# Moving the scaling and storing of the first row half one period earlier, and the pooled sums of a unit ahead of the gating of the one before

## The reference

```python
for g, w in enumerate(POOL_SIZES):            # 2, 4, 8, 16; 128 channels each
    upper = c[:, 1:]                          # c: running sum of the mixer's input
    lower = jnp.pad(c, ((0, 0), (w - 1, 0), (0, 0)))[:, :S]
    outs.append((upper - lower) / cnt - xg[:, :, g])
y = jnp.einsum('bsgd,gde->bsge', pooled, w_pool).reshape(B, S, C_WIDTH) * scale
...
x = x + jnp.einsum('bse,ed->bsd', mix, w_out[l])
return _rmsnorm(x, final_g)                   # needs the squares of a whole row
```

## Time and profile before

| what | value |
|---|---|
| median of 3 runs | 1189.27 us (1188.85 to 1189.97) |
| the profiled execution, its own time | 1189.71 us |
| its span in the trace | 1187.9 us |
| PE busy | 1169.2 us, 98% of the span |
| DVE busy | 872.3 us, 73% |
| ACT busy | 491.5 us, 41% |
| DMA | 354.98 MB, 299 GB/s in the mean |
| mean granted clock of PE | 0.996 of full speed |

### The profile page before, as it was taken

The page is one execution under the profiler, slowest core; times in us unless marked ns, Lnnn a source line. Parts: engine busy times, 40 slices in busy tenths (PEclk is TensorE's granted clock), DMA queues, the critical chain, the costliest instruction groups (busy, mean ns, idle before and its releaser), DMA issues.

```text
span 1187.9 us, 15646 instructions
## 1 busy us (share of the span) xinstructions
PE 1169.2 (98%) x5862; PEld 954.5 (80%) x5862; DVE 872.3 (73%) x1150; ACT 491.5 (41%) x863; POOL 37.5 (3%) x76
## 2 busy tenths in 40 slices
PE   9999999999999999999999999999999999999995
PEld 8878878888888888888888877778878888888884
DVE  5799939677777767888776797988777445586674
ACT  6375564524534333447333362423333432223235
POOL 0012100000000000000000000000000000000000
PEclk9999999999999999999999999999999999999998
DMA  9999999687864476996567686799997648896878
GB/s 349 418 375 415 394 416 346 203 308 286 320 226 160 163 268 243 347 341 202 190 231 261 206 336 232 255 323 363 420 412 302 248 175 342 321 413 226 310 280 326
DMA packets 103435, 354.98 MB, mean 299 GB/s; under 512 B 10656, under 2 KB 17856, under 8 KB 92224
## 3 DMA queue, kind: packets, MB, share of 16 engines
q1 hardware_dynamic: 98432, 336.15, 76.7%
q0 software_dynamic: 4928, 17.83, 3.7%
HBM read 282.37 MB, written 71.57 MB: 298 GB/s over the span
## 4 chain that ended last, share of the span: by engine, by line
PE 81%; DVE 9%; DMA 7%; issue 1%; SPq 1%; ACT 1%; POOL 0%; DVEq 0%; ACTq 0%
PE n_bank L1911 25%; PE n_bank L1912 25%; PE n_bank L1913 25%; DMA x_parts<-s_ring 3%; PE e_bank L2062 2%; DVE w_lo L1344 2%; PE t_bank L2090 2%; PE t_bank L2073 2%; DMA xc<-x_t_dram 2%; DVE w_b L1469 1%; DMA s_ring<-m_parts 1%; DMA s_ring<-x_parts 1%; DVE s_ring L1353 1%; DMA xa<-x_t_dram 1%; DVE va L1526 0%
## 5 line engine op out<-in xcount | busy, mean ns | idle before, releaser
L1006 ACT ACTIVATE w_hi<-w_b 128x1024 fp32r<-128x1024 f32 (+1 forms) x200 | 197.8, 1033 | 421.1 <-PE n_bank L1913 365.3
L1911 PE MATMUL n_bank<-s_ring,w_hi 128*128 128x512 f32 x896 | 357.5, 399 | 1.3 <-DMA s_ring<-x_parts 1.3
L1913 PE MATMUL n_bank<-s_ring,w_lo 128*128 128x512 f32 x896 | 349.0, 390 | 0.0
L1912 PE MATMUL n_bank<-s_ring,w_hi 128*128 128x512 f32 x896 | 349.0, 389 | 0.0
L1344 DVE TENSOR_TENSOR w_lo<-w_b,w_hi 128x1024 fp32r<-128x1024 f32 (+1 forms) x200 | 231.9, 1198 | 102.9 <-ACT w_hi L1006 102.7
L1911 PE MATMUL n_bank<-w_hi,s_ring 128*128 128x512 f32 x672 | 262.1, 390 | 2.0 <-DMA s_ring<-m_parts 0.9
L1913 PE MATMUL n_bank<-w_hi,s_ring 128*128 128x512 f32 x672 | 261.5, 389 | 0.0
L1912 PE MATMUL n_bank<-w_lo,s_ring 128*128 128x512 f32 x672 | 261.5, 389 | 0.0
L1911 PEld LDWEIGHTS n_bank<-s_ring,w_hi 128*128 128x128 f32 x896 | 168.2, 188 | 41.7 <-issue 2.5
L1913 PEld LDWEIGHTS n_bank<-s_ring,w_lo 128*128 128x128 f32 x896 | 168.2, 188 | 35.7
L1912 PEld LDWEIGHTS n_bank<-s_ring,w_hi 128*128 128x128 f32 x896 | 168.3, 188 | 35.3 <-issue 2.2
(11 more groups left out here) (210 smaller groups left out, 945.3 us busy)
## 6 DMA issues: line engine op xcount, KB each, us to landing
s_ring<-x_parts SPq DMA_DIRECT2D x224, 512.0 KB, 6.0
w_b<-w_b_dram SPq DMA_DIRECT2D x76, 1024.0 KB, 10.6
s_ring<-m_parts SPq DMA_DIRECT2D x96, 512.0 KB, 6.1
x_parts<-s_ring POOLq DMA_DIRECT2D x32, 512.0 KB, 11.4
x_parts<-s_ring SPq DMA_DIRECT2D x24, 512.0 KB, 14.5
m_parts<-stage SPq DMA_DIRECT2D x20, 512.0 KB, 8.6
rows<-x_dram SPq DMA_DIRECT2D x8, 1024.0 KB, 11.3
residual<-x_dram SPq DMA_DIRECT2D x6, 1024.0 KB, 9.5
```

The lines of the kernel that those rows point to most:

```text
L1006: sc.activation(w_hi[:, J % 2, part], w_source(J)[:, part], ACT.Copy).then_inc(hi_done, 1)
L1911: pe.matmul(psum_out, stat[0], mov[0], start=first, stop=False)
L1912: pe.matmul(psum_out, stat[0], mov[1], start=False, stop=False)
L1913: return pe.matmul(psum_out, stat[1], mov[0], start=False, stop=last)
```

## The change

`finish_first` moves on ACT from the end of step 96 to step 95, right behind `split_hi(96)`, and on DVE from the end of step 96 to step 95, right behind `split_lo(96)` and ahead of the weight sum and the adds. On SP the four stores of the first half move from the end of step 96's turn to the end of step 95's, which has `load_s(97)` before it and step 96's residual load behind it. In pooling, `pool_half(u + 1)` is called ahead of `pool_gate(u)`, and its wait for PE's reading of `aux` stands just ahead of the write of `aux`, no longer ahead of the window sums.

```diff
@@ SP
-                if n == CHUNKS - 2:
+                if n == CHUNKS - 3:
 
                     for c, y, done, count in ((0, y11[PAIR_O], y_scaled, 4), (1, y12[PAIR_O], y_scaled, 8),
                                               (2, y11[PAIR_O + 1], y_normed, 4), (3, y12[PAIR_O + 1], y_normed, 8)):
@@ ACT
                 elif J + 1 < TOTAL and J not in SUM_S3:
                     split_hi(J + 1)
+                if J == step(PAIR_U, 11):
+                    finish_first()
...
-                if J == step(PAIR_O + 1, 12):
-                    finish_first()
@@ DVE, pool_half
-                if u >= 1:
-                    ve.wait_ge(pool_ready, u)
                 window = POOLS[j]
                 src = pool_x
                 for m in range(j + 1):
...
                     src = dst
+                if u >= 1:
+                    ve.wait_ge(pool_ready, u)
                 last = ve.scalar_tensor_tensor(out=aux[:], in0=src[:, HIST:HIST + HS], scalar=1.0 / window,
@@ DVE, the loop
                 if STEPS <= J + 1 < TOTAL:
                     split_lo(J + 1)
+                if J == step(PAIR_U, 11):
+                    finish_first()
...
                 u = J - POOL_AT
+                if 0 <= u + 1 < 8:
+                    pool_half(u + 1)
                 if 0 <= u < 8:
                     pool_gate(u)
-                if 0 <= u + 1 < 8:
-                    pool_half(u + 1)
...
-                if J == step(PAIR_O + 1, 12):
-                    finish_first()
```

## The result

The changed kernel takes 1196.65 us (median of 4 runs, 1196.44 to 1197.86); the kernel before, run beside it, 1189.11 us. The ratio is 1.0069, with a 95% interval of 1.0056 to 1.0082: slower, by 7.5 us between the medians. The forecast was 1196.0 us, 6.7 us more. The profiled execution has a span of 1194.9 us where 1194.6 was worked out.

What follows compares the result with a forecast made beforehand. PE is busy 98%, but the end is a store backlog. Residual landing 1173.7 + 7.5 + 0.9 + 11.1 + 1.4 = 1194.6 span, +6.7 us, so 1189.27 + 6.7 = 1196.0 us; range 1189.0 to 1198.5.

Steps and rivals of the forecast that it cites:

- The order in SP's queue, and the landing: SP's last residual load waits behind four stores, 4.19 MB or 11.1 us, so its landing moves from 1162.6 to 1173.7.
- From the residual to the end: After the last residual lands: 7.5 us chain, 0.9 to busy DMA, 11.1 of stores, 1.4 to the end; landing + 20.9.
- The term of 7.5 us: DVE and ACT, sixth residual add to the second half's first store: adds, squares, root and scaling, as before, 7.5 us.
- DVE's part and PE's stall: Moved block takes 4.0 us on DVE in step 95; PE stalls 0.1 and 1.9 us, covered by the late residual.
- the fourth rival: Tail: stall's clock or slower root eats the 6 us cover, or stores run at 0.35; 1199 to 1201 us; chance 0.04.
- Pooling: DVE's order of pooled tile and gate gains 0, within 0.1 us either way; PE's wait stays 1.0 us.
- the load passes the stores: Rival at the last residual load: it lands before 1167.0, stores follow without a hole; 1186.9 us at best; chance 0.08.
- it shares the engines with them: Rival: the residual load passes the stores in part, landing 1166 to 1170; 1188.3 to 1192.3 us; chance 0.12.
- The third: Rival: residual near 1164, only PE's stall matters, 3.5 us plus some 2 us of clock; 1189 to 1191 us; chance 0.04.
- the two ceilings: For the four stores' rate: 435 GB/s for the fabric, about 358 for a core's memory; the forecast took 0.376 MB a us.

Runs made afterwards that it cites:

- the run with the residual first: Changed kernel with the four first-half stores put back behind the last residual load, scaling staying in step 95; 1188.69 us, ratio 0.9998.
- the run with the order alone: Kernel before, with only SP's four stores put ahead of the last residual load in step 96's turn, scaling and pooling untouched; 1201.91 us, ratio 1.0107.
- the run on POOL's queue: Changed kernel with the last residual load issued by POOL on its own queue, with its own semaphore; 1190.75 us, ratio 1.0015.
- the cut version: Kernel before, with root and ACT's scaling moved to step 95, DVE's scaling left in step 96, residual load first; 1186.94 us, ratio 0.9984.

## Why the prediction was right

**The order in SP's queue, and the landing.** 1173.7 was forecast, 1173.6 measured. The mechanism is shown from both sides: restoring the order alone gives the time back, making the order alone costs 12.9 us (with SP's wait for the scaling in it), and the same load in another queue is early. The size hit partly by luck, because errors cancel. The execution reached step 95 0.9 us earlier, so that the landing, counted from there, came 0.8 us later than forecast. The slots' loads of step 97, which SP had issued ahead of the stores, ran at only 0.274 and 0.244 MB a us from 1154 to 1158, against 0.379 and 0.344 in the kernel before; the last of them landed at 1159.9, when by the earlier start it should have been 1159.0. Behind them the stores ran at 0.409, where I took 0.376. Against the slower start stands the faster rest. That SP would be held in issuing was not in the forecast; as the load queued behind the stores anyway, it is not seen to have cost anything.

**From the residual to the end.** 20.9 us forecast, 21.3 measured. The term of 7.5 us from the add to the first store came out at 7.5 (1173.58 to 1181.10), and so did 0.9 to a busy DMA; the bytes took 11.2 for 11.1 (1182.0 to 1193.2), and the rest is in the last one, 1.7 us (1193.2 to 1194.9) for 1.4. Counted from the start of step 95 the end came 1.2 us later than forecast, 0.8 of it in the landing and 0.4 in this term; the execution's earlier start hides 0.9, which leaves the span 0.3 us above the forecast. The median is 0.65 us above it, less than the four runs lie apart (1.4 us).

**DVE's part and PE's stall.** The block took 3.9 us (1145.34 to 1149.25) for 4.0: ACT did load its table before it was needed, at 1144, and its scales ended 1.75 us before its next split, where 1.7 was worked out. PE waited 0.17 and 1.60 us where 0.1 and 1.9 were worked out. The granted clock stayed at 1.00 through the wait, so the clock's share of the fourth rival was nothing. The wait was covered by the late residual, as said; once the residual was early it was the next thing to set the end, seen in the run with the residual first. There I had priced the gain of the earlier stores without setting the chain from PE's last bank against it, and so missed by 1 us.

**Pooling.** Forecast at 0 with 0.1 us either way for the instructions; measured 0.2 us more on PE, and PE's wait of step 60, forecast to stay at 1.0 us, became 1.27. Its mechanism stands: PE needs both, and the later one decides.

**The rivals.** That the load passes the stores is ruled out by the run with the order alone; that it shares the engines with them is how it goes between two queues, but not within one. Its price (L near 1166 to 1170, 1188.3 to 1192.3 us) is what the run on POOL's queue gave, 1190.75. The third needed a residual that is not late; the run with the residual first has that and the same stall of PE, and it took 1188.7 us, since the stall was 1.8 us and not 3.5 and cost no clock. The fourth is out as well: the last bank's add came only at 1183.8, behind the residual's chain, with the cover not used up, and the stores ran at 0.41; what was slow, for 0.9 us in all, were the slots' loads.

For the order in one queue say more than the prediction took from them. By the two landings alone the loads could also have shared the engines, which were full then. But the weight load between them landed at 892.1 (880.23 + 11.9), 2.4 us behind the store and 2.5 us ahead of the load of u: one after the other.

## What to carry to other kernels

Before a store is moved ahead, look at what is queued behind it on the same issuer: a load that the critical path still needs then waits for all its bytes, here 4.2 MB and 11 us, and, if the store itself must wait for its data, for that too. The wait shows in the trace of a far-off engine. Put the load first, or give it a queue of its own, and only then look for the gain. And take an early finish apart: the part on an idle engine (ACT's scales) could move for nothing, while the part on DVE pushed the weights of the next step by 3.9 us (their split starts 16.9 us behind ACT's split of step 95, before 13.0).

## What the runs showed of the hardware that I had not expected

Stores of the same shape ran at two rates. Where they followed loads without a pause, they went at 0.40 to 0.41 MB a us: 409 GB/s in the changed kernel from 1160 to 1166, 408 in the cut version at 1170 to 1172, with a DMA share of 1.05. Where they started on idle engines they went at 0.36 to 0.39: 376 GB/s in the changed kernel after 1182, and all through the backlog of the kernel before (384 at 1176 to 1178). The faster rate is above the lower of the two ceilings from which the prediction made its estimates; the measured rate decides. No run here tells the cause of the two rates.

Loads slowed down when stores stood behind them in the same queue. From 1154 to 1158 the changed kernel moves at 274 and 244 GB/s. These are still the slots' loads of step 97: they land by 1159.9 and the first store only at 1162.5, 2.6 us before the second. So of the 10 us by which the stores are issued earlier, only 5 are left at the first landing (1167.5 in the kernel before). Over the same windows these loads ran at 379 and 344 GB/s in the kernel before and at 326 and 381 with the residual first, where no store is issued by then; with the residual on its own queue, where the stores stand behind them again, at 266 and 227. Why is not shown.

SP takes longer over an issue when much is under way: the two stores from 1154.19 took it 5.2 us and the residual load 2.5, where the residual load took 0.4 us in the kernel before. No semaphore accounts for it, since the tiles of these stores were scaled by 1149.3 and the fifth residual add was done by 1157.7. What SP waits for in it is not shown.
